# Opening, modulation schedule and norm placement of a two-block transformer kernel on one core

## The chip, the cores and the metric

The kernel runs on one core of a Trainium2 chip. The metric is the device time of one execution in microseconds (us), the median of three runs. The engines are TensorE (PE, products and transposes), VectorE (DVE), ScalarE (ACT), GpSimd (POOL, which here only issues DMAs) and SyncE (SP, which issues the weight DMAs).

## The reference

Two transformer blocks run one after the other on 256 tokens of width 1024, in float32. The first has two layers of "macaron" form, the second two layers on the same stream with a second (context) stream beside it.

```python
def first_block(x, c, ada_w, ada_b, norm_g, ...):
    c_act = jax.nn.silu(c)
    for l in range(2):
        mod = c_act @ ada_w[l] + ada_b[l]                    # 9 vectors of 1024 a layer
        sh1, sc1, g1, sh2, sc2, g2, sh3, sc3, g3 = jnp.split(mod, 9, axis=-1)
        n1 = modulate(rms_norm(h, norm_g[l, 0]), sh1, sc1)   # x * (1 + scale) + shift
        h = h + 0.5 * g1 * swiglu(n1, ...)                   # d_ff 2816
        n2 = modulate(rms_norm(h, norm_g[l, 1]), sh2, sc2)
        h = h + g2 * token_mixing(n2, ...)                   # two kinds of attention, gates, w_o
        n3 = modulate(rms_norm(h, norm_g[l, 2]), sh3, sc3)
        h = h + 0.5 * g3 * swiglu(n3, ...)
    return rms_norm(h, final_g)
# second block: layer 0 projects both streams with ev_w_in (1024 x 3104), runs gated scans;
# layer 1 is window attention; each with an MLP of 4096; its modulation vectors are
# silu(c) @ w_mod + b_mod and silu(c_ctx) @ w_mod + b_mod, 6 vectors of 1024 a layer and stream
```

## The kernel before, in words

**Weights.** Every weight matrix is cut into chunks of 1 MB (128 x 2048 float32). SP loads chunk n into `stage` (a ring of three), ACT rounds it into `whi`, DVE subtracts to get the rest `wlo` (both are `conv(n)`), and PE multiplies with both halves. A chunk of a projection is 48 products, of a feed-forward stage 32 wide pairs. The stages and their chunk counts stand in `PHASES`: F0 (first feed-forward), in0, gate0, out0 (token mixing), F1, F2, in1, gate1, out1, F3, then evc and evx (the "even inputs" of the context and the latent stream, 12 chunks each), evoc, evox, Mc, M0 (MLPs), odc, odx, odo, M1. DVE's conv of chunk n + 2 stands in window n of each stage, so DVE and ACT run two chunks ahead of PE, and each must wait until PE has used a chunk (`chunk_used`).

**Modulation vectors.** One vector is 8 steps on DVE: `mod_steps` multiplies a 128 x 1024 slice of the weight by a column of silu(c) and adds it to an accumulator (L1773, L1776). POOL loads the weight in quarters of 1 MB into `modw` (two buffers; the first eight, c = 0 to 7, have rooms of their own where possible) and one quarter feeds two steps. After 8 steps PE transposes the accumulator (`turn_mod`, 8 transposes, L742), and DVE sums and adds the bias (`take_mod`, L1784). The table `VECTORS` says which stage makes which vectors, `STEPS` and `EVEN_STEPS` how many steps stand in each window, `EVEN_TURNS` after which chunk of an even input PE turns a vector. PE stands still at a turn until DVE has done the 8 steps.

**Opening.** SP loads 11 rows of parameters and three small broadcasts (13 DMAs), ACT the identity, c, the other constants (772 KB) and x, POOL eight quarters: vector ada(0, 1) (the scale of the first norm) and ada(0, 0) (its shift). PE turns the parameters, turns x, sums the squares for the first norm (`rms_stat("n0")`), turns the scale vector, then the shift vector, and after `keep_warm` (products that keep PE busy, L633) the first chunk of F0.

**Norms.** A norm's mean square comes from 8 products with a matrix of ones (`column_sums`), whose squares ACT makes (`squares`) and whose root ACT and DVE take. n2 and n5 follow the out stages; the key n6 (the first block's last norm) is worked out inside evc, lc0 (a layer norm of the context stream) inside evx: this is the "other stream's norm" of the even inputs.

Of the kernel before, what the change touches and what calls it, by code (L numbers as in the profile page):

```python
# [42 lines left out]
def shape_constants():  # L43
# [21 lines left out]
    base = np.concatenate([ident, ones, blk, rot, sel_even, sel_odd, tri_f, tri_b, tri_s, pos_f, pos_b, cols], 1)  # L65
# [21 lines left out]
for _name, _width in (("ident", P), ("ones", P), ("blk", P), ("rot", P), ("sel_even", P), ("sel_odd", P),  # L87
                      ("tri_f", P), ("tri_b", P), ("tri_s", P), ("pos_f", T), ("pos_b", T), ("cols", 8)):
    CONST_AT[_name] = (_at, _width)
    _at += _width  # L90
BASE_W = _at
TABLE_W = 4 * T
# [25 lines left out]
def program(nc, A, out_ap, book):  # L118
    ctx = ExitStack()
    with ctx:  # L120
# [36 lines left out]
        hidden_table = same_room("hidden_table", "table", [P, 4 * 256], F32R)  # L157
        plain_xs = same_room("plain_xs", "xs", [P, KB, T], F32)
# [69 lines left out]
        def wmod(l, v, which):  # L228
# [11 lines left out]
            "out1": [ada(1, 8)],  # L240
            "F3": [wmod(0, 2, 2)] + [wmod(0, v, 1) for v in range(3)],
# [12 lines left out]
        NMOD = len(mods)  # L254

        def mc(key, k=0, n=1):
# [3 lines left out]

        macc_arena = arena[:, 43 * 256:47 * 256]
        macc_even = hid[:].rearrange("p s f t -> p (s f t)")[:, 0:1024]

        start_room = {c: arena[:, 4096 + 2048 * (c - 2):4096 + 2048 * (c - 1)] for c in (2, 3, 4)}
        start_room.update({5: nraw[:].rearrange("p b t -> p (b t)"), 6: stage[:, 2, :]})
        quarter = lambda c: start_room.get(c, modw[:, c % 2, :])
        macc_of = lambda m: macc_even if m == 1 or mod_first["evc"] <= m < mod_first["Mc"] else macc_arena
# [4 lines left out]
            "F1": [0] + 22 * [1] + 4 * [2] + [2, 0, 1, 1, 0, 0],  # L272
            "Mc": [0] + 15 * [1] + [1, 0, 2, 0, 0, 2, 2, 0, 0, 2, 2, 0, 2, 2, 2, 0],
            "M1": [0, 0] + 8 * [1] + 22 * [0],
            "out0": 4 * [0] + [2, 2, 2, 0],
        }
        for name, like in (("F2", "F0"), ("F3", "F1"), ("M0", "Mc"), ("out1", "out0")):
            STEPS[name] = STEPS[like]
        turn_at, step_n = {}, 16
        for name in ("F0", "in0", "out0", "F1", "F2", "in1", "out1", "F3", "evc", "evx", "Mc", "M0", "M1"):  # L280
# [31 lines left out]
        param_landed = sem("param_landed")  # L312
# [16 lines left out]
        nparam = 16 * (len(wide_rows) + 8)  # L329
# [74 lines left out]
        EVEN_TURNS = {"c": (4, 7, 10), "x": (4, 9)}  # L404
        EVEN_STEPS = {"c": (2, 0, 2, 2, 2, 2, 3, 3, 2, 3, 3, 0), "x": (2, 2, 2, 1, 1, 2, 2, 2, 1, 1, 0, 0)}
# [9 lines left out]
        def _(sp):  # L415
# [6 lines left out]
            for at, n, src in ((0, 16, A["od_sink_2"].rearrange("a h -> (a h)")), (16, 8, A["ev_ret_theta_2"].rearrange("a b c -> (a b c)")),  # L422
                               (24, 512, A["lam_p"].rearrange("a b c -> (a b c)"))):
                sp.dma_start(small[:, at:at + n], src.partition_broadcast(P)).then_inc(param_landed, 16)
# [21 lines left out]
            def ffn(name, l, i):  # L446
                n = first[name]
                g, u, d = A["ffn_wg"][l, i], A["ffn_wu"][l, i], A["ffn_wd"][l, i]
                for j in range(PAIRS):
                    load(n + 2 * j, cols(g, j))  # L450
                    load(n + 2 * j + 1, cols(u, j))
                    if name == "F0" and j == 0:
                        sp.wait_ge(mod_step, 14)
# [44 lines left out]
            sp.wait_ge(mod_step, 10)  # L498
# [32 lines left out]
        def _(pool):  # L531
            for m, (w, l, v, _, _, _) in enumerate(mods):
                for q in range(4):
                    c = 4 * m + q
                    src = w[l].rearrange("(k p) n -> p k n", p=P)[:, 2 * q:2 * q + 2, v * 1024:(v + 1) * 1024]
                    if c < 8:

                        if c == 7:
                            pool.wait_ge(mod_step, 4)
                        pool.dma_start(quarter(c).rearrange("p (a b) -> p a b", a=2), src).then_inc(start_landed[c], 16)  # L540
                        continue
# [3 lines left out]
                if m == 1:  # L545
                    pool.wait_ge(pe_out.sem, pe_out.at(("turned", 0)))
                    pool.wait_ge(mod_step, 12)
                    pool.dma_start(arena[:, 2048:4096].rearrange("p (a d) -> p a d", a=2),
                                   A["ctx_2"].rearrange("b (a p) d -> p (b a) d", p=P)).then_inc(ctx_landed, 16)
# [3 lines left out]
        def _(pe):  # L553
# [227 lines left out]
            def rms_stat(key):  # L781
# [3 lines left out]
                if key != "n0":  # L785
                    keep_warm(R[:, 1, :], 8 if key == "n1" else 16 if key in JOINED else 22)
# [23 lines left out]

            pe.wait_ge(param_landed, nparam)
# [3 lines left out]
            turn_rows(0)  # L815
            rms_stat("n0")
            pe.wait_ge(act_out.sem, act_out.at("cact"))
            turn_mod(0, R[:, 2:4, :])
            pe.wait_ge(mod_step, 14)
            pe.wait_ge(act_out.sem, act_out.at(("turned", 0)))  # L820
            keep_warm(Y[:, 0, :], 10)
            turn_mod(1, R[:, 2:4, :])
            keep_warm(Y[:, 0, :], 12)

            def mixer(l):
# [60 lines left out]
                for c in range(9):  # L886
# [9 lines left out]
                    if c == 3:  # L896
                        if l == 0:
                            pe.wait_ge(act_out.sem, act_out.at(("turned", 1)))
# [84 lines left out]
            def even(which):  # L983
# [6 lines left out]
                if which == "c":  # L990
                    column_sums(other)
                else:
                    mean_sums(other, other_res)
                for c in range(12):
# [4 lines left out]
                    if c == 1:  # L999
# [5 lines left out]
                        last.then_inc(pe_out.sem, pe_out.next(("lr", which)))  # L1005
                    if which == "x" and c == 3:
                        column_sums(other)
                    if c == 4:
# [252 lines left out]
        def _(act):  # L1261
# [27 lines left out]
            def ffn(name):  # L1289
# [22 lines left out]
                for w in range(24, 33):  # L1312
                    conv(n + w + 2)
                    if w == 28 and key is not None:
                        squares(key, resx, lambda h: (key, "res", h), (0, 1))
                    if w == 29 and name == "F3":
# [26 lines left out]
            def squares(key, src, ready, parts=range(4)):  # L1343
                if 0 in parts:
# [51 lines left out]
            def rms(key, target, l, i):  # L1396
                if key != "n0":
                    squares(key, resx, lambda h: (key, "res", h), (2, 3) if key in JOINED else range(4))
# [8 lines left out]
            act.dma_start(base[:, 0:P], A["const"][:, 0:P]).then_inc(ident_landed, 16)  # L1407
# [3 lines left out]
            act.dma_start(base[:, P:BASE_W], A["const"][:, P:BASE_W]).then_inc(param_landed, 16)  # L1411

# [3 lines left out]
            done(f(cact[:].rearrange("p a k -> p (a k)"), R[:, 2, 0:3 * KB], ACT.Silu), "cact")  # L1416
            def take_rows(s, res):
# [4 lines left out]
            squares("n0", resx, None)  # L1422
            root("n0", eps6)
            act.wait_ge(dve_out.sem, dve_out.at("lamdot"))
            done(f(stat[:, 0:4], stat[:, 0:4], ACT.Exp), "lamexp")
            act.wait_ge(dve_out.sem, dve_out.at("small"))
            link(f(ec("theta"), ec("theta"), ACT.Exp))
            done(f(ec("lg_all"), ec("theta"), ACT.Ln, scale=-1.0, bias=one), "lg")
            conv(0)
            conv(1)  # L1430

# [1041 lines left out]
```

## Time and profile before

| | |
|---|---|
| Median of 3 runs | 2349.35 us (2348.09 to 2349.47) |
| Profiled execution, its own time | 2350.69 us |
| Its span, first to last instruction | 2348.9 us |
| PE busy | 2227.6 us (95%) |
| DVE busy | 1771.9 us (75%) |
| ACT busy | 1155.4 us (49%) |
| DMA mean | 215 GB/s |

The profiled execution took 1.3 us longer than the median. PE is busy almost always, so what counts is the time in which it is not, and where it runs at the lower clock.

### The profile page before, as it was taken

What the parts mean: (1) busy time and instruction counts of PE and PEld (TensorE: products, weight loads), DVE (VectorE), ACT (ScalarE), POOL (GpSimd) and SP (SyncE); (2) the same over time, 40 slices, a digit from 0 to 9 for tenths busy, and PEclk for the clock granted to TensorE, in tenths of its full rate; (3) what the DMA queues carried; (4) which work ended last, traced back from release to release, by engine and by line L of the source; (5) the groups of instructions that cost most, each with busy time, mean ns of one, the idle gap of its engine ahead of it and who ended that gap; (6) DMA issues with size and microseconds to landing.
All of it is one profiled execution on the core that took longest, in us unless ns stands there. A gap on an engine that the chain in (4) does not pass through costs nothing.

```text
span 2348.9 us, 33801 instructions
## 1 busy us (share of the span) xinstructions
PE 2227.6 (95%) x14278; PEld 1943.2 (83%) x14294; DVE 1771.9 (75%) x2092; ACT 1155.4 (49%) x1443; POOL 109.5 (5%) x157
## 2 busy tenths in 40 slices
PE   4999999999999999999998788999999999999998
PEld 3888889788888889988888677878888888768886
DVE  6888776888788877688886676667878877686763
ACT  2554556444355455645534334436635733485742
POOL 1000000000000000000000000000000000000000
PEclk8999999999999999999999999999999999999999
DMA  8889654688878865458877515607778877304651
GB/s 309 269 279 320 216 180 144 200 275 286 279 233 279 300 227 180 154 189 277 278 268 243 208 52 187 214 19 251 256 263 271 277 242 259 108 3 146 211 195 56
DMA packets 330446, 505.22 MB, mean 215 GB/s; under 512 B 12327, under 2 KB 239878, under 8 KB 330295
## 3 DMA queue, kind: packets, MB, share of 16 engines
q1 hardware_dynamic: 288071, 340.70, 44.0%
q0 software_dynamic: 41616, 160.44, 19.7%
q8 instruction: 113, 1.85, 0.3%
q10 hardware_dynamic: 608, 1.92, 0.2%
q14 instruction: 38, 0.31, 0.0%
HBM read 501.98 MB, written 1.05 MB: 214 GB/s over the span
## 4 chain that ended last, share of the span: by engine, by line
PE 86%; DVE 8%; ACT 3%; issue 2%; DMA 1%; SPq 0%; ACTq 0%; DVEq 0%
PE banks L576 36%; PE banks L577 18%; PE banks L568 7%; PE banks L570 6%; PE banks L569 6%; PE banks L795 2%; PE banks L742 2%; PE banks L633 2%; PE banks L769 2%; DVE wlo L1749 1%; PE banks L778 1%; ACT whi L1283 1%; DVE hid L1776 1%; DMA arena<-in_lam_p_dram 1%; DVE arena L1776 0%
## 5 line engine op out<-in xcount | busy, mean ns | idle before, releaser
L1749 DVE TENSOR_TENSOR wlo<-stage,whi 128x2048 fp32r<-128x2048 f32 (+1 forms) x326 | 737.0, 2261 | 187.4 <-ACT whi L1283 186.7
L1283 ACT CAST whi<-stage 128x2048 fp32r<-128x2048 f32 x322 | 615.4, 1912 | 365.7 <-PE banks L577 281.9
L576 PE MATMUL banks<-xs,whi 128*128 128x512 f32 x2176 | 763.0, 396 | 3.0 <-DVE xs L1940 1.6
L577 PE MATMUL banks<-xs,wlo 128*128 128x256 f32 x2176 | 607.1, 279 | 0.0
L576 PEld LDWEIGHTS banks<-xs,whi 128*128 128x128 f32 x2176 | 408.2, 188 | 100.4 <-issue 2.9
L568 PE MATMUL banks<-xs,whi 128*128 128x256 f32 x1440 | 417.9, 290 | 11.6 <-DVE xs L1940 7.9
L577 PEld LDWEIGHTS banks<-xs,wlo 128*128 128x128 f32 x2176 | 410.0, 188 | 0.1
L569 PE MATMUL banks<-xs,whi 128*128 128x256 f32 x1440 | 409.1, 284 | 0.0
L570 PE MATMUL banks<-xs,wlo 128*128 128x256 f32 x1440 | 408.9, 284 | 0.0
L576 PE MATMUL banks<-hidden_arena,whi 128*128 128x512 f32 x992 | 354.3, 399 | 0.0
L568 PEld LDWEIGHTS banks<-xs,whi 128*128 128x128 f32 x1440 | 278.0, 193 | 22.5 <-issue 10.5
L1776 DVE SCALAR_TENSOR_TENSOR arena<-modw,cact,arena 128x1024 f32<-128x1024 f32 x220 | 281.8, 1281 | 9.3 <-DMA modw<-in_ada_w_dram 6.1
L577 PE MATMUL banks<-hidden_arena,wlo 128*128 128x256 f32 x992 | 278.8, 281 | 0.0
L569 PEld LDWEIGHTS banks<-xs,whi 128*128 128x128 f32 x1440 | 278.0, 193 | 0.9 <-issue 0.5
L570 PEld LDWEIGHTS banks<-xs,wlo 128*128 128x128 f32 x1440 | 277.7, 193 | 0.0
L576 PEld LDWEIGHTS banks<-hidden_arena,whi 128*128 128x128 f32 x992 | 186.5, 188 | 45.1
L577 PEld LDWEIGHTS banks<-hidden_arena,wlo 128*128 128x128 f32 x992 | 186.3, 188 | 0.1
L576 PE MATMUL banks<-hs,whi 128*128 128x512 f32 x336 | 120.3, 396 | 0.0
L544 POOL DMA_DIRECT2D modw<-in_w_mod_dram x80 | 57.1, 714 | 1174.7 <-DVE arena L1776 887.3
L577 PE MATMUL banks<-hs,wlo 128*128 128x256 f32 x336 | 94.0, 280 | 0.0
L544 POOL DMA_DIRECT2D modw<-in_ada_w_dram x64 | 45.7, 714 | 868.9 <-DVE arena L1776 846.2
L1303 ACT COPY hid<-banks 128x512 f32<-128x512 f32 x44 | 25.8, 587 | 120.1 <-PE banks L577 120.1
(320 smaller groups left out, 2492.6 us busy)
## 6 DMA issues: line engine op xcount, KB each, us to landing
stage<-in_mlp_w_dram SPq DMA_DIRECT2D x96, 1024.0 KB, 5.4
modw<-in_w_mod_dram POOLq DMA_DIRECT2D x80, 1024.0 KB, 5.8
modw<-in_ada_w_dram POOLq DMA_DIRECT2D x67, 1024.0 KB, 5.7
stage<-in_ffn_wg_dram SPq DMA_DIRECT2D x44, 1024.0 KB, 5.5
stage<-in_ffn_wu_dram SPq DMA_DIRECT2D x44, 1024.0 KB, 7.5
stage<-in_ffn_wd_dram SPq DMA_DIRECT2D x44, 1024.0 KB, 7.4
stage<-in_ev_w_in_dram SPq DMA_DIRECT2D x24, 1024.0 KB, 6.0
stage<-in_w_in_dram SPq DMA_DIRECT2D x18, 1024.0 KB, 5.7
```

Source lines behind the costliest of these rows:

```text
L544: pool.dma_start(modw[:, c % 2, :].rearrange("p (a b) -> p a b", a=2), src).then_inc(mod_landed[c % 2], 16)
L568: mm(out, hi, xh, start=first_mm, stop=False, skip_group_check=True)
L569: mm(out, hi, xl, start=False, stop=False, skip_group_check=True)
L570: return mm(out, lo, xh, start=False, stop=last_mm, skip_group_check=True)
L576: mm(out, hi, pair.rearrange("p a t -> p (a t)"), start=first_mm, stop=False, skip_group_check=True)
L577: return mm(out[:, 0:T], lo, pair[:, 0, :], start=False, stop=last_mm, skip_group_check=True)
L633: mm(bank, zero.to_broadcast([P, P]), zero.to_broadcast([P, 512]), start=True, stop=True)
L742: last = nc.tensor.transpose(banks[:, k // 4, (k % 4) * P:(k % 4 + 1) * P], macc_of(m)[:, k * P:(k + 1) * P], ident)
L769: last = mm(out, ones, src[:, k, :], start=k == 0, stop=k == 7, skip_group_check=True)
L1283: nc.scalar.copy(whi[:, s, :], stage[:, s, :]).then_inc(hi_done, 1)
L1749: last = v.tensor_tensor(wlo[:, s, at], stage[:, s, at], whi[:, s, at].bitcast(F32), ALU.subtract)
L1776: v.scalar_tensor_tensor(out=acc, in0=w, scalar=cc, in1=acc, op0=ALU.mult, op1=ALU.add).then_inc(mod_step, 1)
```

## The change

In the opening the shift vector is no longer made by DVE. Its four quarters stay where they land (two of them in rooms that are free then, `plain_hs` and `plain_xs`), and PE multiplies each 128 x 128 block by one column of silu(c), 64 products that add up in eight columns of one bank. DVE adds the bias. ACT loads x right after c and the rest of the constants only after conv(1). PE turns x first and the parameters after it, turns the scale vector ahead of the norm's sums, and conv(0) on ACT stands ahead of the norm's root. SP waits for quarter 3 before chunk 0, for quarter 5 before chunk 1 and for the end of the one-column products before chunk 2; POOL waits for that too before the context stream and the next quarters. Small scalar work moves into F0.

The out stages lose their six steps each to F1 and F3. Of evc's three vectors one goes to Mc, of evx's two one goes on; Mc and M0 have five vectors instead of four. ACT makes n2's and n5's squares bank by bank in the out stage, and `keep_warm` behind these norms is 16 instead of 22. The other stream's norm stands one or two chunks later in the even inputs, and the turns after chunks 5 and 9 (evc) and 9 (evx) instead of 4, 7, 10 and 4, 9.

```diff
         VECTORS = {
-            "start": [ada(0, 1), ada(0, 0)],
+            "start": [ada(0, 1)],
...
-            "out0": [ada(0, 8)],
-            "F1": [ada(1, v) for v in range(4)],
+            "F1": [ada(0, 8)] + [ada(1, v) for v in range(4)],
...
-            "evc": [wmod(0, v, 2) for v in range(3, 6)],
-            "evx": [wmod(0, 3, 1), wmod(0, 4, 1)],
-            "Mc": [wmod(0, 5, 1), wmod(1, 0, 2), wmod(1, 1, 2), wmod(1, 0, 1)],
-            "M0": [wmod(1, v, 1) for v in range(1, 5)],
+            "evc": [wmod(0, 3, 2), wmod(0, 4, 2)],
+            "evx": [wmod(0, 3, 1)],
+            "Mc": [wmod(0, 5, 2), wmod(0, 4, 1), wmod(0, 5, 1), wmod(1, 0, 2), wmod(1, 1, 2)],
+            "M0": [wmod(1, v, 1) for v in range(5)],
...
-            "Mc": [0] + 15 * [1] + [1, 0, 2, 0, 0, 2, 2, 0, 0, 2, 2, 0, 2, 2, 2, 0],
+            "Mc": [0] + 3 * [1, 1, 2, 1, 1] + [1, 0, 2, 2, 0, 2, 2, 2, 0, 2, 2, 0, 2, 2, 3, 0],
...
-        EVEN_TURNS = {"c": (4, 7, 10), "x": (4, 9)}
-        EVEN_STEPS = {"c": (2, 0, 2, 2, 2, 2, 3, 3, 2, 3, 3, 0), "x": (2, 2, 2, 1, 1, 2, 2, 2, 1, 1, 0, 0)}
+        EVEN_TURNS = {"c": (5, 9), "x": (9,)}
+        EVEN_STEPS = {"c": (1, 2, 2, 0, 2, 1, 2, 2, 2, 2, 0, 0), "x": (1, 1, 0, 1, 1, 0, 1, 1, 1, 1, 0, 0)}
...
+            keep_warm(Y[:, 3, :], 12)
+            turn_rows(0)
             pe.wait_ge(param_landed, nparam)
...
-            turn_rows(0)
-            rms_stat("n0")
             pe.wait_ge(act_out.sem, act_out.at("cact"))
             turn_mod(0, R[:, 2:4, :])
-            pe.wait_ge(mod_step, 14)
+            rms_stat("n0")
             pe.wait_ge(act_out.sem, act_out.at(("turned", 0)))
-            keep_warm(Y[:, 0, :], 10)
-            turn_mod(1, R[:, 2:4, :])
-            keep_warm(Y[:, 0, :], 12)
+            for t in range(8):
+                if t % 2 == 0:
+                    pe.wait_ge(start_landed[4 + t // 2], 16)
+                for k in range(KB):
+                    last = mm(Y[:, 0, k:k + 1], quarter(4 + t // 2)[:, (t % 2) * 1024 + k * P:(t % 2) * 1024 + (k + 1) * P],
+                              cact[:, 0, t:t + 1], start=t == 0 and k == 0, stop=t == 7, skip_group_check=True)
+            last.then_inc(pe_out.sem, pe_out.next("shift0"))
+            keep_warm(Y[:, 1, :], 12)
...
-            act.dma_start(base[:, P:BASE_W], A["const"][:, P:BASE_W]).then_inc(param_landed, 16)
...
             squares("n0", resx, None)
+            conv(0)
             root("n0", eps6)
...
-            conv(0)
             conv(1)
+            act.dma_start(base[:, FIRST_W:BASE_W], A["const"][:, FIRST_W:BASE_W]).then_inc(base_landed, 16)
...
                 for c in range(4, 8):
                     conv(n + c + 2)
+                    if c >= 5:
+                        squares(key, resx, lambda h: (key, "res", h), (c - 5,))
...
             def start_shift():
                 conv(0)
-                mod_steps(2)
-                take_mod(R[:, 2:4, :])
+                dve.wait_ge(pe_out.sem, pe_out.at("shift0"))
+                link(v.tensor_tensor(mc(shift0[5], 0, 8), Y[:, 0, 0:8], pcol[:, shift0[4]:shift0[4] + 8], ALU.add))
```

On PE the whole opening of before, up to the first product of F0 (L576; L795 are transposes of c, the parameters and x, L769 the norm's sums, L742 the turns of a modulation vector, L633 keep_warm):

```order
L795 MATMUL banks<-base,table 128x24
L795 MATMUL banks<-base,arena 128x49 x8
L795 MATMUL banks<-base,arena 128x7
L795 MATMUL banks<-base,arena 128x128 x16
L769 MATMUL banks<-resc,base 128x256 x8
L742 MATMUL banks<-base,arena 128x128 x8
L633 MATMUL banks<-base 128x512 x10
L742 MATMUL banks<-base,hid 128x128 x8
L633 MATMUL banks<-base 128x512 x12
L576 MATMUL banks<-xs,whi 128x512
```

and of the change (its lines are one or more further down; L826 are the one-column products, whose four rooms are the four quarters):

```order
L796 MATMUL banks<-base,table 128x24
L634 MATMUL banks<-base 128x512 x12
L796 MATMUL banks<-base,arena 128x128 x16
L796 MATMUL banks<-base,arena 128x49 x8
L796 MATMUL banks<-base,arena 128x7
L743 MATMUL banks<-base,arena 128x128 x8
L770 MATMUL banks<-resc,base 128x256 x8
L826 MATMUL banks<-cact,arena 128x1 x16
L826 MATMUL banks<-cact,plain_hs 128x1 x16
L826 MATMUL banks<-cact,stage 128x1 x16
L826 MATMUL banks<-cact,plain_xs 128x1 x16
L634 MATMUL banks<-base 128x512 x12
```

The scale vector's turn now stands ahead of the sums, and 64 one-column products stand where the shift vector's turn stood.

On DVE the middle of evc, before, from window 3 to the turn's take after chunk 7 (L1749 is the lo half of a chunk, L1773 and L1776 are steps, L1784 and L1786 the take of a vector, L2256 a part of the scan's gate):

```order
L1776 SCALAR_TENSOR_TENSOR hid<-modw,cact,hid 128x1024 x2
L1749 TENSOR_TENSOR wlo<-stage,whi 128x2048
L1776 SCALAR_TENSOR_TENSOR hid<-modw,cact,hid 128x1024 x2
L2256 SCALAR_TENSOR_TENSOR arena<-banks,arena 128x1024
L1749 TENSOR_TENSOR wlo<-stage,whi 128x2048
L1784 TENSOR_REDUCE mcol<-banks 128x8
L1786 TENSOR_TENSOR mcol<-mcol,pcol 128x8
L1773 TENSOR_SCALAR hid<-modw,cact 128x1024
L1776 SCALAR_TENSOR_TENSOR hid<-modw,cact,hid 128x1024
L1749 TENSOR_TENSOR wlo<-stage,whi 128x2048
L1776 SCALAR_TENSOR_TENSOR hid<-modw,cact,hid 128x1024 x3
```

and of the change, from the end of the norm (L1982 writes the normed stream) to the first steps of the second vector:

```order
L1982 SCALAR_TENSOR_TENSOR resx<-resx,pcol,arena 128x256 x8
L1761 TENSOR_TENSOR wlo<-stage,whi 128x2048
L1788 SCALAR_TENSOR_TENSOR hid<-modw,cact,hid 128x1024 x2
L2268 SCALAR_TENSOR_TENSOR arena<-banks,arena 128x1024
L1761 TENSOR_TENSOR wlo<-stage,whi 128x2048
L1788 SCALAR_TENSOR_TENSOR hid<-modw,cact,hid 128x1024
L1761 TENSOR_TENSOR wlo<-stage,whi 128x2048
L1796 TENSOR_REDUCE mcol<-banks 128x8
L1798 TENSOR_TENSOR mcol<-mcol,pcol 128x8
L1785 TENSOR_SCALAR hid<-modw,cact 128x1024
L1788 SCALAR_TENSOR_TENSOR hid<-modw,cact,hid 128x1024
```

The first vector's eighth step now stands one chunk later, alone in its window, and the norm stands right ahead of it.

## Rows read from the trace of the kernel before

**Rows 1.** The page, busy time of each engine over the span.

```profile
PE 2227.6 (95%) x14278; PEld 1943.2 (83%) x14294; DVE 1771.9 (75%) x2092; ACT 1155.4 (49%) x1443; POOL 109.5 (5%) x157
```

**Rows 2.** Stretches: us, busy of PE, PEld, DVE, ACT, POOL, PE clock, DMA share, GB/s.

```profile
8.00:19.00 11.00, 0.12 (x1) 0.00 (x0) 4.61 (x4) 0.19 (x1) 0.71 (x1) 1.00 0.98 377
...
1300.00:1350.00 50.00, 38.69 (x296) 35.15 (x299) 28.90 (x40) 17.30 (x20) 3.57 (x5) 0.90 0.53 186
```

**Rows 3.** Timeline of PE in the opening: start, length in us, idle before.

```profile
27.83 6.56 PE L769 MATMUL banks<-resc,base 128*128 128x256 f32 x16 [3.90 <-ACT resc L1357]
...
49.29 1.97 PE L742 MATMUL banks<-base,hid 128*128 128x128 f32 x8 [6.20 <-DVE hid L1776]
51.05 4.27 PE L633 MATMUL banks<-base 128*128 128x512 bf16 x12
54.97 0.58 PE L576 MATMUL banks<-xs,whi 128*128 128x512 f32 x1
```

**Rows 4.** DMA issues of the first 26 us: KB each, us to landing.

```profile
arena<-in_ada_w_dram POOLq DMA_DIRECT2D x3, 1024.0 KB, 18.1
...
arena<-in_x_dram ACTq DMA_DIRECT2D x1, 1024.0 KB, 14.4
...
base<-in_const_dram ACTq DMA_DIRECT2D x1, 772.0 KB
```

**Rows 5.** DMA queues from 1242 to 1244 us: packets, MB, share of 16 engines.

```profile
q0 software_dynamic: 131, 0.47, 60.4%
q1 hardware_dynamic: 289, 0.30, 42.5%
```

**Rows 6.** Groups on PE of the first 60 us, shapes apart: busy us, mean ns.

```profile
L795 PE MATMUL banks<-base,arena 128*128 128x128 f32 x16 | 3.3, 390 | 0.0
...
L795 PE MATMUL banks<-base,arena 49*128 49x49 f32 x8 | 1.1, 308 | 11.3 <-DMA arena<-in_lam_p_dram 11.3
```

**Rows 7.** Timeline of PE in the even inputs.

```profile
1237.55 5.38 PE L769 MATMUL banks<-arena,base 128*128 128x256 f32 x16 [2.71 <-ACT arena L1357]
...
1275.79 1.69 PE L742 MATMUL banks<-base,hid 128*128 128x128 f32 x8 [4.81 <-issue]
...
1300.13 1.97 PE L742 MATMUL banks<-base,hid 128*128 128x128 f32 x8 [4.44 <-DVE hid L1776]
...
1327.67 1.97 PE L742 MATMUL banks<-base,hid 128*128 128x128 f32 x8 [7.69 <-DVE hid L1776]
...
1422.80 3.62 PE L778 MATMUL banks<-resc,base 128*128 128x256 f32 x16
...
1464.69 1.94 PE L742 MATMUL banks<-base,hid 128*128 128x128 f32 x8 [6.77 <-issue]
```

**Rows 8.** Timeline of DVE in evc.

```profile
1270.88 2.29 DVE L1749 TENSOR_TENSOR wlo<-stage,whi 128x2048 fp32r<-128x2048 f32 x1 [2.33 <-ACT whi L1283]
...
1297.47 2.61 DVE L1776 SCALAR_TENSOR_TENSOR hid<-modw,cact,hid 128x1024 f32<-128x1024 f32 x2 [1.24 <-DMA modw<-in_w_mod_dram]
```

**Rows 9.** Waits of PE over the span: us in total, times, longest.

```profile
PE banks L766 <- ACT nraw L1351: 6.6, 2, 3.3
```

**Rows 10.** Timeline of PE at the norm n2 (end of out0).

```profile
435.73 0.59 PE L761 MATMUL banks<-nraw,base 128*128 128x256 f32 x2
...
442.79 6.63 PE L633 MATMUL banks<-base 128*128 128x512 bf16 x21 [0.22 <-issue]
449.07 0.58 PE L576 MATMUL banks<-xs,whi 128*128 128x512 f32 x1
```

**Rows 11.** Timeline of DVE at the norm n2.

```profile
434.80 2.60 DVE L1776 SCALAR_TENSOR_TENSOR arena<-modw,cact,arena 128x1024 f32<-128x1024 f32 x2
...
439.51 0.87 DVE L1902 SCALAR_TENSOR_TENSOR resx<-banks,ecol,resx 128x256 f32<-128x256 f32 x2
...
451.12 0.88 DVE L1996 SCALAR_TENSOR_TENSOR xs<-nraw,mcol,xs 128x256 fp32r<-128x256 f32 x2 [0.19 <-ACT xs L1390]
```

**Rows 12.** Timeline of DVE in Mc, after window 18.

```profile
1708.34 2.29 DVE L1749 TENSOR_TENSOR wlo<-stage,whi 128x2048 fp32r<-128x2048 f32 x1 [3.27 <-ACT whi L1283]
```

More of the change, by code:

```diff
@@ L91 @@
 BASE_W = _at
+FIRST_W = 2 * P + 8
 TABLE_W = 4 * T
@@ L785, in rms_stat @@
                 if key != "n0":
-                    keep_warm(R[:, 1, :], 8 if key == "n1" else 16 if key in JOINED else 22)
+                    keep_warm(R[:, 1, :], 8 if key == "n1" else 16)
             def ln_stat(key, res):
@@ L1005, in even @@
                         last.then_inc(pe_out.sem, pe_out.next(("lr", which)))
+                    if which == "c" and c == 1:
+                        column_sums(other)
+                    if which == "x" and c == 1:
+                        mean_sums(other, other_res)
                     if which == "x" and c == 3:
                         column_sums(other)
-                    if c == 4:
+                    if c == EVEN_TURNS[which][0]:
                         pe.wait_ge(dve_out.sem, dve_out.at((other, "rooted")))
@@ L1315, in ffn @@
                         squares(key, resx, lambda h: (key, "res", h), (0, 1))
+                    if w == 24 and name == "F0":
+                        act.wait_ge(base_landed, 16)
+                        act.wait_ge(dve_out.sem, dve_out.at("lamdot"))
+                        done(f(stat[:, 0:4], stat[:, 0:4], ACT.Exp), "lamexp")
+                        link(f(ec("theta"), ec("theta"), ACT.Exp))
+                        done(f(ec("lg_all"), ec("theta"), ACT.Ln, scale=-1.0, bias=one), "lg")
                     if w == 29 and name == "F3":
@@ L1343, in squares @@
             def squares(key, src, ready, parts=range(4)):
-                if 0 in parts:
+                if 0 in parts and key != "n0":
                     nc.scalar.preload_act_table_set(LN_EXP)
@@ L1565, in even @@
                         done(nc.scalar.copy(E["lr"][32:48, :], R[32:48, 3, 0:T]), ("lr", which))
-                        if which == "c":
-                            root(other, eps6)
-                    if c == 3 and which == "x":
+                    if c == 2 and which == "c":
+                        root(other, eps6)
+                    if c == 4 and which == "x":
                         root(other, eps5)
@@ L1819, in ffn @@
                     j = w // 2
+                    if name == "F0" and w == 2:
+                        lam_dots()
                     if w % 2 == 1:
@@ L1831, in ffn @@
                         residual_half(name, key, resx, lambda k: ec("g2x", k, 1), 0)
-                    if name == "F0" and w == 23:
+                    if name == "F0" and w == 26:
                         scalars()
@@ L2085, in _, with lam_dots @@
             done(v.tensor_copy(pcol[:, 8 * nwide:8 * nwide + 7], R[:, 1, 8 * nwide:8 * nwide + 7]), "pcol")
-            mod_steps(4)
             own("pcol")
             take_mod(R[:, 2:4, :])
-            mod_steps(2)
+            def lam_dots():
+                dve.wait_ge(small_landed, 48)
+                lam = small[:, 24:536].rearrange("p (x a n) -> p x a n", x=4, a=2)
+                prod = arena[:, 1700:1956].rearrange("p (x n) -> p x n", x=4)
+                link(v.tensor_tensor(prod, lam[:, :, 0, :], lam[:, :, 1, :], ALU.mult))
+                link(v.tensor_reduce(stat[:, 0:4], prod, AX_X, ALU.add))
+                v.tensor_scalar(ec("sink"), small[:, 0:16], -1.0, None, ALU.mult)
+                done(v.tensor_copy(ec("theta"), small[:, 16:24]), "lamdot")
             def scalars():
@@ L2243, in even @@
                     conv(n + c + 2)
-                    if which == "c" and c == 1:
+                    if which == "c" and c == 3:
                         final_norm(other)
-                    if which == "x" and c == 0:
+                    if which == "x" and c == 2:
                         ln_center(other, other_res)
-                    if which == "x" and c == 3:
+                    if which == "x" and c == 5:
                         ln_finish(other, other_res, 0, 0)
```

106 lines of the change are left out of this document (46 added, 60 removed).

## The prediction

> **What bounds the kernel now.** I read the page first: PE is busy for 2227.6 of 2348.9 us [rows 1]. The reader is to see that PE's 121 idle us are nearly all there is to win, beside the stretches in which it runs at its lower level. Stretches of 50 us show where they lie: the first 55 us, two gaps at the ends of the out stages, and the even inputs, where PE is busy for 38.7 of 50 us and the mean granted clock is 0.90, a mix of the levels 2.4 and 1.2 GHz [rows 2]. Elsewhere PE is all but full, and DVE has 6 to 10 us of 50 free there. Then the timelines of PE, DVE and ACT in these three places tell which wait ends last.
>
> In the opening it is this: PE sums the squares (6.56 us), stands until DVE has the shift vector's eight steps, turns it at 49.29, runs keep_warm, and F0's first product starts at 54.97 [rows 3]. In evc PE stands three times at a turn, 4.81, 4.44 and 7.69 us, and once, 2.71 us, for the squares of the other stream's norm; in evx once, 6.77 us [rows 7]. At n2 and n5 it stands for the last squares, 3.3 us each [rows 9].
>
> **Opening: what the change costs there.** The one-column products are the unknown. First, when may they begin? Of the DMAs, quarters 2 to 4 took 18.1 us in the median from issue (3.5 us), so quarter 3's landing was near 21.6 us; 772 KB of constants no longer go ahead of x and the quarters [rows 4], which at 377 GB/s [rows 2] is 2 us. So quarter 3 lands near 19.7, two steps of 1.3 each (two in 2.61, [rows 8]) end at 22.3, the turn (1.97, rows 3, at the lower clock, since PE has stood idle ahead of it) ends at 24.3, and the sums, 6.56 as before, at 30.9. x lands much earlier than its 17.3 (2.9 + 14.4) and isn't late for this.
>
> Then 64 float32 products. A float32 product has two rows in the trace (L769: 8 products, 16 rows), so 128 passes, each with its own load of 128 columns of weights. No row shows a one-column pass. The nearest are the float32 transposes of the opening [rows 6]: 128 columns wide 3.3 / 16 = 0.21 us each, 49 wide 1.1 / 8 = 0.14. The 79 columns between cost 0.07; one column would be 0.10 on that line, 0.14 if the load of the weights sets the pace from 49 columns on. I take 0.12: 128 x 0.12 = 15.4 us, end at 46.3. Bounds: 0.06, half of it, if PE is at its upper level (the transposes' pace fits the lower one), and 0.21, the widest row. Quarter 7 isn't late: the 11.6 MB of all quarters, x, parameters and two chunks take some 29 us at 377 to 400 GB/s behind a start of 4 us, so it lands near 33 to 35. From the turn's end (51.26) to F0's first product before were 3.7 us, set by keep_warm. So F0 starts near 50.0, **5.0 us earlier**. The other chain doesn't come last: chunk 0 lands at 30 to 34 (SP's small packets get 0.30 MB while POOL's get 0.47 [rows 5]), ACT's half of it ends two later, root, refinement, eight products and the lo half on DVE end near 41 to 44, and the first split needs 1.5 more.
>
> The Trainium skill, page "TensorE: Matmul & The Clock Gate", section "LDWEIGHTS (loading the stationary operand)", gives columns / 1.2 ns for a load of weights, 107 ns for 128 columns. By it 128 passes would be 13.7 us, a gain of 6.7. The section "Wait — 56ns, not 53.3ns?" of that page gives a floor of 25 ns, or 62 with decode in software; by that alone they would be 3 to 8 us.
>
> What the new waits give back: chunk 2 is asked for only at 46.3, together with chunk 3, the context stream and two quarters, 5 MB at once, where before chunk 2 was long there. By rows 5's shares chunk 2 lands near 54 and chunk 3 near 62. PE wants them 11.3 and 17 us after F0's start, at 61.3 and 67, with 4.2 us of ACT and DVE ahead of it, and DVE's small products (moved to window 2) and up-gate stand in between. Chunk 3 is late by about **1.5 us** (0 to 6); what hides the rest is PE's work on chunks 0 to 2.
>
> **evc.** Three gaps and the squares, 19.65 us [rows 7], go; the new order leaves two waits. Turn after chunk 5: DVE's lo half of chunk 6 starts at 1270.88 [rows 8] for the same reason as before (ACT's part of the gate). Behind it on DVE: itself 2.2, two steps 2.6, the gate's subtraction 1.2, the next lo 2.2, one step 1.3, so 1280.4. Chunk 4 ended at 1275.79 - 4.81 = 1270.98; a chunk is 6.0 us (from turn to turn 24.34, less 1.69 and 4.44, over three; 5.8 without the slow one behind a turn). So PE stands 3.5 us. Turn after chunk 9: the turn of before after chunk 7 stood 4.44 with three steps; one step less is 1.3, and 1.24 of it was a late quarter [rows 8], now asked for earlier: 1.7 left. So 14.4 us less idle. The sums took 5.38 where the same 16 passes took 3.62 in evx [rows 7], as they follow a gap: 1.8. Slow products behind a turn: about 0.7 each time, and one turn fewer with its 2.0: 4 in all with what goes at the gap removed. **evc: 20 us.** That the norm stands two windows later costs nothing: it is read only in evox's stage and its room only at the first turn, and DVE had 2.3 us idle in the place it takes and still ends ahead of ACT's late half.
>
> **evx.** 6.77 us idle, the turn 2.0, and a chunk that took 1.7 more at the lower clock behind them; left 0.3 to 0.6 at the turn after chunk 9 with one step in its window. **evx: 10 us.**
>
> **n2, n5.** Of n2: DVE's last residual starts at 439.51, though PE's last chunk ended at 435.73 (where the norm's own sums begin), because the pair sum waited for ACT's squares behind three casts, and two steps (2.60) and a lo half followed it [rows 10, 11]. With squares bank by bank and without steps it starts at 435.7: 3.8 less, and 0.6 more as the last sums follow no gap. keep_warm (6.63 for 21) ended later than the split was ready; with 16, and no lower clock, it ends before. The last piece of the split ended at 452.0 and then comes 4.4 earlier, 447.6, with two blocks' products (1.4) behind: the first chunk of F1 ends at 449.0 and not 449.07 + 5.65. **n2: 5.7**, n5 by its rows of the same kind (its sums were at the upper level) **4.7**.
>
> **What it moves.** 28 steps of 1.3 us go to F1, F3 (6 each), Mc and M0 (8 each), into windows with spare DVE time: in Mc, at window 19, DVE stood 3.27 us before its next lo half [rows 12] and gets two steps, 2.6. Their cover gone, each would cost 1.3. Not covered: the last window of Mc and M0, three steps for two just ahead of a turn, 1.3 each at most (I take 1.2); F3's window 30, 0.7; the two vectors' turns, 1.0 each at the upper level. **Loss 5.1 us.**
>
> **Sum**: 5.0 - 1.5 + 20 + 10 + 5.7 + 4.7 - 5.1 = 38.8, from 2350.69 is 2311.9; the profiled run was 1.3 over the median, so **2310.5 us**.
>
> **Rivals.**
> (A) One-column passes cost 0.2 or more, as wide transposes do. For it: PE does little in them, and all float32 transposes of the opening were slow; against: those move 128 columns through the array and these one. F0 then starts at 30.9 + 26.9 + 3.7 = 61.5, 6.5 later than before: sum 27, 2322.
> (B) Passes at 0.06 or less. The DVE chain then bounds, F0 at 43 to 45: 2304 to 2305. The skill's floor of 25 to 62 ns on the page named above would be this case.
> (C) The moved steps are not hidden: DVE is busy 39 to 44 of 50 us in those stages, and at half price they give 18 back: 2325. Against it: the idle 3.27 of rows 12, and two chunks of lead.
> (D) Slower than before: one-column passes don't overlap at all, since all add into one bank, and each takes its whole recorded length; L769's at the lower clock is 6.6 / 16 as pace but 0.31 to 0.6 as length (rows 6 have 0.31 and 0.39). At 0.6 they are 77 us, F0 starts at 111, 56 later: sum -17, 2368. It decides from (38.8 + 15.4) / 128 = 0.42 us a pass.
> (E) The change doesn't do it: the turns wait as long one chunk later, since steps and norm were only reordered. Then evc and evx give 10 in place of 30: 2330. Against it: steps per window ahead of each turn fell from three to two and one.
>
> **How the numbers follow.** My forecast 0.62, A 0.12, B 0.10, C 0.07, E 0.06, D 0.03. No more than 2 in 10 outside: 2300 to 2326 leaves out D, E and the far ends. Within 0.2% (4.7 us, about what a measurement of this kernel can tell from no change) of 2349.35 lies only a thin part of D and E: 0.02. Slower 0.02, faster 0.96.
>
> **What would show it.** Right: L826's rows about 0.12 apart; F0's first product near 50; PE's waits at turns in evc about 3.5 and 1.7, none of note in evx; n2's and n5's idle 3.3 gone; one small wait near F0's chunk 3. Wrong: passes far from 0.12, a wait of PE on lo halves in F0 over 6 us, or new waits at turns in Mc, M0, F1 or F3.

## The result, and the profile after

The changed kernel took 2335.81 us (median of 4 runs, 2334.38 to 2339.74), the kernel before, beside it, 2348.72 us. The ratio is 0.9942, 95% interval 0.9927 to 0.9957: by the ratio 13.6 us faster where 38.8 were forecast, and outside the range of 2300 to 2326. The profiled execution of the changed kernel was its longest, 2339.74 us with a span of 2338.0, so between the two spans lie 10.9 us.

To find where these went, I took the start of the same product in both timelines of PE and noted by how much the gap between the two kernels changed from one such mark to the next (positive is time saved):

| Stretch | Forecast | Measured |
|---|---|---|
| up to F0's first product (54.97, now 57.67) | 5.0 | -2.7 |
| F0's chunks 0 to 3 (fifth chunk 77.77, now 84.14) | -1.5 | -3.7 |
| n2 with the first two chunks of F1 | 5.7 | 5.5 |
| the rest of F1, up to n5 | 0 | -1.1 |
| n5 with the first two chunks of F3 | 4.7 | 4.0 |
| the rest of F3 | -0.7 | -1.9 |
| evc with its stage of scans | 20 | 20.3 |
| evx | 10 | 10.6 |
| evox | 0 | 1.9 |
| Mc | -2.2 | -9.4 |
| M0 | -2.2 | -10.2 |
| the rest | 0 | -2.4 |
| sum | 38.8 | 10.9 |

So the even inputs and the norms gave what was forecast. Of the 27.9 us between forecast and measurement 15.2 lie in the two MLPs, 7.7 in the stretch up to F0 and 2.2 in F0's first chunks. The page, busy time of each engine after:

```profile
PE 2243.5 (96%) x14388; PEld 1960.2 (84%) x14404; DVE 1759.6 (75%) x2083; ACT 1158.2 (50%) x1445; POOL 109.5 (5%) x157
```

PE's busy time grew by 15.9 us [rows 1]: a busy engine isn't a useful one, and 23.8 of it are the one-column products. The timeline of PE in the opening, to be laid beside [rows 3]:

```profile
23.92 1.94 PE L743 MATMUL banks<-base,arena 128*128 128x128 f32 x8 [6.45 <-DVE arena L1788]
25.65 4.12 PE L770 MATMUL banks<-resc,base 128*128 128x256 f32 x16
29.61 3.63 PE L826 MATMUL banks<-cact,arena 128*128 128x1 f32 x32
33.10 6.62 PE L826 MATMUL banks<-cact,plain_hs 128*128 128x1 f32 x32
39.58 6.97 PE L826 MATMUL banks<-cact,stage 128*128 128x1 f32 x32
46.41 6.96 PE L826 MATMUL banks<-cact,plain_xs 128*128 128x1 f32 x32
53.61 4.41 PE L634 MATMUL banks<-base 128*128 128x512 bf16 x11 [0.24 <-issue]
57.67 0.59 PE L577 MATMUL banks<-xs,whi 128*128 128x512 f32 x1
...
76.86 0.50 PE L577 MATMUL banks<-xs,whi 128*128 128x512 f32 x1 [1.90 <-DVE hid L1823]
```

The first 32 passes take 3.49 us from their start to that of the next ones, 0.109 us each; the other 96 take 0.20 to 0.22. Windows of 2 us on PE (us, busy, granted clock, DMA share, GB/s) show why:

```profile
30.00:32.00 2.00, 2.00 (x20) 1.00 1.08 359
32.00:34.00 2.00, 2.00 (x18) 0.87 1.10 350
34.00:36.00 2.00, 2.00 (x11) 0.50 0.49 156
...
44.00:46.00 2.00, 2.00 (x11) 0.50 0.00 0
```

PE is busy without a gap, and yet its granted clock falls from 2.4 to 1.2 GHz. The last number matters too: from 42 to 54 us the DMA queues are empty, since SP waits for these products before it asks for chunk 2.

The timeline of PE at the turns, beside [rows 7]: evc's two, evx's one, and the last ones of Mc and M0:

```profile
1275.69 1.72 PE L743 MATMUL banks<-base,hid 128*128 128x128 f32 x8 [3.72 <-issue]
...
1302.90 1.10 PE L743 MATMUL banks<-base,hid 128*128 128x128 f32 x8 [1.57 <-DVE hid L1788]
...
1466.53 1.06 PE L743 MATMUL banks<-base,hid 128*128 128x128 f32 x8 [0.29 <-issue]
...
1753.51 1.94 PE L743 MATMUL banks<-base,arena 128*128 128x128 f32 x8 [5.89 <-issue]
...
1952.85 1.94 PE L743 MATMUL banks<-base,arena 128*128 128x128 f32 x8 [6.17 <-issue]
```

The first three are as forecast (3.5, 1.7 and 0.3 to 0.6). The last two are new. DVE in windows 28 to 30 of Mc, just ahead of the first of them, beside [rows 12]:

```profile
1736.77 2.67 DVE L1788 SCALAR_TENSOR_TENSOR arena<-modw,cact,arena 128x1024 f32<-128x1024 f32 x2
1739.37 2.28 DVE L1761 TENSOR_TENSOR wlo<-stage,whi 128x2048 fp32r<-128x2048 f32 x1
1741.57 1.28 DVE L1788 SCALAR_TENSOR_TENSOR arena<-modw,cact,arena 128x1024 f32<-128x1024 f32 x1
1744.01 1.28 DVE L1788 SCALAR_TENSOR_TENSOR arena<-modw,cact,arena 128x1024 f32<-128x1024 f32 x1 [1.17 <-DMA modw<-in_w_mod_dram]
1745.21 2.29 DVE L1761 TENSOR_TENSOR wlo<-stage,whi 128x2048 fp32r<-128x2048 f32 x1
1747.41 1.28 DVE L1788 SCALAR_TENSOR_TENSOR arena<-modw,cact,arena 128x1024 f32<-128x1024 f32 x1
1750.80 2.60 DVE L1788 SCALAR_TENSOR_TENSOR arena<-modw,cact,arena 128x1024 f32<-128x1024 f32 x2 [2.11 <-DMA modw<-in_w_mod_dram]
```

Steps stand 2, 1 + 1, 1 + 2 here: the last vector had one step in window 26, so its first three quarters (two steps each) are split between two windows. And POOL, which issues the quarters:

```profile
1744.63 0.72 POOL L550 DMA_DIRECT2D modw<-in_w_mod_dram  x1 [5.56 <-issue]
```

`modw` has two rooms, so the last quarter can be asked for only when the step that ended at 1742.85 has freed one. It is asked for at 1744.63 and DVE has it at 1750.80, while PE has stood since 1747.62. In M0 the two waits for a quarter are 1.39 and 2.16 us.

### The profile page after: what moved, and what is told of

It reads as the page before. It is cut to its first block, busy times and chain, and to the rows that moved or that the text cites. A ratio compares the mean times of both kernels' runs of the same rounds, so it can differ in the third digit from the quotient of the medians.

```text
span 2338.0 us, 34014 instructions
## 1 busy us (share of the span) xinstructions
PE 2243.5 (96%) x14388; PEld 1960.2 (84%) x14404; DVE 1759.6 (75%) x2083; ACT 1158.2 (50%) x1445; POOL 109.5 (5%) x157
## 4 chain that ended last, share of the span: by engine, by line
PE 85%; DVE 9%; ACT 3%; issue 2%; DMA 1%; POOL 0%; ACTq 0%; DVEq 0%; SPq 0%; POOLq 0%
PE banks L577 35%; PE banks L578 18%; PE banks L569 7%; PE banks L571 7%; PE banks L570 7%; PE banks L796 2%; PE banks L743 2%; DVE wlo L1761 1%; PE banks L770 1%; PE banks L826 1%; PE banks L779 1%; PE banks L634 1%; DVE arena L1788 1%; DMA stage<-in_ffn_wu_dram 1%; DMA arena<-in_ada_w_dram 1%
## 5 line engine op out<-in xcount | busy, mean ns | idle before, releaser
L1788 DVE SCALAR_TENSOR_TENSOR arena<-modw,cact,arena 128x1024 f32<-128x1024 f32 x234 | 299.8, 1281 | 23.3 <-DMA modw<-in_w_mod_dram 15.7
```

The lines of the kernel that those rows point to most:

```text
L1788: v.scalar_tensor_tensor(out=acc, in0=w, scalar=cc, in1=acc, op0=ALU.mult, op1=ALU.add).then_inc(mod_step, 1)
```

## The experiments

Ratios are to the kernel before, run on the same chip beside each; the changed kernel's own is 0.9942. A hundredth is 23.5 us, and the intervals reach 0.0012 to 0.0015 to either side.

### The two halves of the change

**The opening undone** (that of before, with everything else as changed):

> The opening of before (shift vector by DVE, constants ahead of x), everything else as changed. Theory: the change's own opening costs time, F0's first product 2.7 us later and chunk 3 of F0 another 3.7 us, so this kernel is 6.4 us faster than the changed one: 2329.4 us, ratio to before 0.992. Rival: the opening gained what was forecast and the loss came from noise between programs: then this kernel is 3.5 us slower than the changed one, 2339.

Measured: 2331.25 us, ratio 0.9912 (0.9897 to 0.9927), F0's first product at 54.10, its fifth chunk at 76.48. The new opening costs some 7 us by the ratios and 7.7 by the fifth chunk's start (84.14): it lost time. The theory held.

**The other stream's norm at its old chunks**, steps and turns as changed:

```diff
                 first_chunk(n, R[:, 0, :], ("ev", which))
+                if which == "c":
+                    column_sums(other)
+                else:
+                    mean_sums(other, other_res)
...
-                    if which == "c" and c == 1:
-                        column_sums(other)
```

> The changed kernel with the other stream's norm back at its old chunks in evc and evx (sums behind chunk 0's first products, DVE's part in windows 1, 0 and 3), steps and turns as changed. Theory: of the 20 us that evc gained, the 2.7 us wait for the squares and some 1.8 us of slow products behind it come from the norm's place, the rest from steps and turns; so 4.5 us slower than the changed kernel, 2340, ratio 0.9961. Rival: the norm's later place is what shortened the waits at the turns, through DVE's windows: then 8 us or more are lost, ratio 0.998 or higher.

Measured: 2341.33 us, ratio 0.9965 (0.9953 to 0.9978), 5.4 us more than the change. The timeline of PE has the old wait again, while the turn's is where it was (3.72 in the changed kernel):

```profile
1236.20 3.69 PE L770 MATMUL banks<-arena,base 128*128 128x256 f32 x16 [2.71 <-ACT arena L1370]
...
1277.35 1.94 PE L743 MATMUL banks<-base,hid 128*128 128x128 f32 x8 [3.65 <-issue]
```

So of evc's 20 us the norm's place is worth about 4 (3.9 by the marks in PE's timeline, 5.4 by the ratios, whose intervals leave several us of room), and the turns the rest; evx saved as much in this kernel as in the changed one.

### The last turns of Mc and M0

**One step moved** from window 30 to window 1 of the changed kernel:

```diff
-            "Mc": [0] + 3 * [1, 1, 2, 1, 1] + [1, 0, 2, 2, 0, 2, 2, 2, 0, 2, 2, 0, 2, 2, 3, 0],
+            "Mc": [0] + [2, 1, 2, 1, 1] + 2 * [1, 1, 2, 1, 1] + [1, 0, 2, 2, 0, 2, 2, 2, 0, 2, 2, 0, 2, 2, 2, 0],
```

> The changed kernel with one step of Mc and M0 moved from window 30 to window 1, so that the last vector starts in window 26 with an even step and no quarter is split between two windows. Theory: the wait of 5.9 us at the last turn of each MLP comes from quarters that are asked for one window late (DVE waits 1.17 and 2.11 us for them) and the slow clock behind it; then 7 to 8 us come back in each of Mc and M0: 2320.5 us (2319 to 2324), waits at the last turns under 0.5 us. Rival: DVE has no time left there and the eight steps cost 1.3 us each wherever they stand: only the third step of window 30 is saved, 1.3 us twice, 2333.

Measured: 2319.88 us, ratio 0.987 (0.9856 to 0.9883): 17 us, by the ratios, from one step moved. The same turns in PE's timeline:

```profile
1747.08 1.06 PE L743 MATMUL banks<-base,arena 128*128 128x128 f32 x8 [1.58 <-issue]
...
1938.71 1.03 PE L743 MATMUL banks<-base,arena 128*128 128x128 f32 x8
```

The first still waits 1.58 where under 0.5 was expected: DVE's timeline has one wait for a quarter left there.

```profile
1744.37 2.61 DVE L1788 SCALAR_TENSOR_TENSOR arena<-modw,cact,arena 128x1024 f32<-128x1024 f32 x2 [1.25 <-DMA modw<-in_w_mod_dram]
```

By the marks Mc and M0 together now lose 4.2 us against the kernel before, where the change lost 19.6 and the forecast had 4.4.

**The kernel before, with the odd step and nothing else:**

```diff
-            "Mc": [0] + 15 * [1] + [1, 0, 2, 0, 0, 2, 2, 0, 0, 2, 2, 0, 2, 2, 2, 0],
+            "Mc": [0] + 15 * [1] + [1, 0, 2, 0, 0, 2, 2, 0, 0, 2, 1, 0, 2, 2, 3, 0],
```

> The kernel before, with one thing changed: in Mc and M0 the last vector has one step in window 26 and three in window 30, in place of two and two. The number of steps and vectors is that of before. Theory: what made the last turns of the changed kernel wait is that every quarter of the last vector is then split between two windows, so that quarter 3's room comes free a window late and its DMA lands after DVE wants it: a wait of about 4.6 us (1.17 and 2.11 for quarters and one step of 1.3) and 2 us of slow products behind it in each MLP, 13 us in all, ratio 1.0055. Rival: the waits came from the fifth vector, which leaves DVE too few free windows: then the one step in window 30 costs 1.3 us twice at most, ratio 1.001.

Measured: 2365.56 us, ratio 1.0058 (1.0045 to 1.007), 13.6 us slower than before. PE waits 5.03 and 4.41 us at the two turns, and DVE's timeline ahead of the first has the same two waits for a quarter as the changed kernel:

```profile
1772.56 1.28 DVE L1776 SCALAR_TENSOR_TENSOR arena<-modw,cact,arena 128x1024 f32<-128x1024 f32 x1 [1.11 <-DMA modw<-in_w_mod_dram]
...
1779.60 2.60 DVE L1776 SCALAR_TENSOR_TENSOR arena<-modw,cact,arena 128x1024 f32<-128x1024 f32 x2 [2.36 <-DMA modw<-in_w_mod_dram]
```

With four vectors and DVE no busier than before, moving one step from window 26 to window 30 makes the wait. The third step in window 30 accounts for 1.3 us of it, the two late quarters for the rest. The rival, too little free time on DVE, is out.

### The one-column products

**A wide product behind every fourth one-column product:**

```diff
+                    if (at * KB + k) % 4 == 3 and (at < 7 or k < 7):
+                        keep_warm(Y[:, 1, :], 1)
```

> The changed kernel with one product of keep_warm (128x512, bf16) behind every fourth one-column product. Theory: the granted clock falls from 1.00 to 0.50 some 4 us into the one-column products because they hardly use the array; with the wide ones it stays, the 128 passes take 0.109 us each as in the first quarter, 14.0 us and 15 x 0.22 = 3.3 us for the wide ones, in place of 23.8: F0 starts 6.5 us earlier, at 51.2, and the time is 2329. Rival: the clock falls all the same and the wide products come on top, 15 x 0.43 = 6.4 us: F0 at 64, 2342.

Measured: 2341.08 us, ratio 0.9957 (0.9945 to 0.997), 3.5 us slower than the change, which the two intervals alone can't tell from nothing. The timeline can: the clock fell all the same, to 0.53 from 34 us on and 0.50 from 36 on, and F0 began at 61.51, 3.8 us later. The rival held, though it had F0 at 64.

**Behind every one:**

> The changed kernel with one product of keep_warm (128x512, bf16) behind every one-column product, 63 in all, half of PE's time if the clock holds. Theory: the clock falls because one-column products count as little work; with half the time wide it holds at 1.00, and the stretch takes 14 + 63 x 0.22 = 27.9 us. Rival: something else pulls the clock down some 6 us after it rose, whatever PE does: then it is at 0.50 from 34 us on, as with every fourth, and the stretch takes over 45 us.

Measured: 2332.28 us, beside a kernel before of 2349.99; this is one run, so only its timeline is read. Windows of PE, the first as the clock had risen:

```profile
28.00:30.00 2.00, 2.00 (x11) 1.00 1.01 385
...
34.00:36.00 2.00, 2.00 (x19) 1.00 0.50 157
...
50.00:52.00 2.00, 2.00 (x19) 1.00 0.00 0
```

And PE's timeline at the end of the stretch:

```profile
52.43 0.28 PE L826 MATMUL banks<-cact,plain_xs 128*128 128x1 f32 x2
52.56 2.78 PE L634 MATMUL banks<-base 128*128 128x512 bf16 x12
55.00 0.58 PE L577 MATMUL banks<-xs,whi 128*128 128x512 f32 x1
```

The clock held at 1.00 throughout, so what pulled it down was the products' kind and not the time since it rose. PE's sequence repeats every 0.354 us; a wide product is 0.22 of that, which leaves 0.07 a pass, less than the 0.109 of a pass among its like. That part of the loads of weights lies behind the wide products would explain it, but isn't shown. The 64 products and 63 wide ones took 22.5 us, not the 27.9 expected, and end at 52.7, 0.7 us before the 64 alone in the changed kernel. keep_warm then takes 2.78 us, not 4.41, and F0 starts 2.7 us earlier, but then waits 2.95 us (1.90 before) for chunk 3, which comes from the next cause.

**Quarter 6 first, and chunk 2 asked for behind its 16 products:**

```diff
-            for t in range(8):
+            for at, t in enumerate((4, 5, 0, 1, 2, 3, 6, 7)):
...
+                if at == 1:
+                    last.then_inc(pe_out.sem, pe_out.next("quarter6"))
...
-                        sp.wait_ge(pe_out.sem, pe_out.at("shift0"))
+                        sp.wait_ge(pe_out.sem, pe_out.at("quarter6"))
```

> The changed kernel with quarter 6, which lies in chunk 2's room, multiplied first of the four, and SP waiting for those 16 products only before it asks for chunk 2. Theory: chunk 3's 1.9 us wait in F0 and the low clock behind it (3.7 us in all) come from chunk 2 being asked for at 53; now it is asked for near 34 and chunk 3 near 45, while the DMA queues are empty, and 3.7 us come back: 2332 us. Rival: the stall is that of ACT and DVE behind the first split, and nothing is gained: 2336. F0's first product stays near 57.7 in both.

Measured: 2332.26 us, ratio 0.992 (0.9906 to 0.9933). F0 starts at 57.21 and its fifth chunk at 80.58, 3.6 us ahead of the changed kernel's, with no gap of PE over 0.4 us in F0's first chunks. The theory held.

### Towards a better kernel

**Aligned steps and early chunk 2 together:**

> Aligned steps in Mc and M0, and quarter 6 first with the early request for chunk 2, together. The two stand at different places, so the savings should add: the ratios of the two alone were 0.987 and 0.992 against 0.9942 of the change, so 0.9848, 2315.5 us beside a kernel before of 2351.3. Rival: part of the saving of the early request was noise between programs: 0.987.

Measured: 2317.75 us, ratio 0.9865 (0.985 to 0.9879). F0's fifth chunk starts at 79.84, against 83.28 with aligned steps alone, so 3.4 us were saved there. The ratio moved by 0.0005 alone: its interval holds the rival's 0.987 and just misses the theory's 0.9848, so the time doesn't confirm that the savings add.

**DVE does half of the shift vector:**

```diff
-            for at, t in enumerate((4, 5, 0, 1, 2, 3, 6, 7)):
+            for at, t in enumerate((4, 5, 6, 7)):
...
+            pe.wait_ge(dve_out.sem, dve_out.at("shift_half"))
+            for k in range(KB):
+                last = mm(Y[:, 0, k:k + 1], macc_even[:, k * P:(k + 1) * P], ones[:, 0:1], start=False, stop=True, skip_group_check=True)
```

> As the one before, and DVE does the four steps of quarters 4 and 5 right behind its take of the scale vector, while PE multiplies quarters 6 and 7 and then DVE's accumulator by a column of ones: 40 products in place of 64, 80 passes. Theory: half the passes still run at the lower clock (0.21 us): the last one ends near 43.5 in place of 53, then DVE's own chain (lo half of chunk 0 to 44.3, then the split) and keep_warm bound, and F0 starts at 48 to 49 in place of 57: 8 us less, ratio 0.9815. Rival: DVE's steps start late, since its chain for the norm stands behind them, and PE waits: F0 at 52, ratio 0.983.

Measured: 2306.57 us, ratio 0.9819 (0.9804 to 0.9834), the fastest of all. PE's timeline:

```profile
28.98 3.63 PE L826 MATMUL banks<-cact,stage 128*128 128x1 f32 x32
32.47 6.20 PE L826 MATMUL banks<-cact,plain_xs 128*128 128x1 f32 x32
38.53 3.55 PE L832 MATMUL banks<-base,hid 128*128 128x1 f32 x16
42.32 4.84 PE L634 MATMUL banks<-base 128*128 128x512 bf16 x11 [0.24 <-issue]
46.66 0.73 PE L577 MATMUL banks<-xs,whi 128*128 128x512 f32 x1
```

F0 starts 11.0 us earlier than in the changed kernel. PE didn't wait for DVE, which had time while PE summed the squares.

**DVE does three quarters of it:**

> As the kernel in which DVE does half of the shift vector, but DVE does three of its four quarters (4, 5 and 7), PE multiplies quarter 6 alone (32 passes) and then DVE's accumulator by ones (16), keep_warm is 26 products, and DVE adds the bias ahead of its lo half of chunk 0. Theory: the shift vector is ready near 37, so ACT's split can start when DVE has normed the first blocks, at 41, and F0 starts at 43.7 in place of 46.7: 3 us less, ratio 0.9806. Rival: ACT's cast of chunk 1 and DVE's chain are no earlier and keep_warm's 26 products end after 46: no gain, 0.982.

Measured: 2308.88 us, ratio 0.9817 (0.9803 to 0.983): nothing gained. The shift vector was ready early, but PE stood 2 us for DVE's last step, the clock was at the lower level, and there keep_warm's products took 8.27 us, up to F0's start:

```profile
35.77 3.58 PE L832 MATMUL banks<-base,hid 128*128 128x1 f32 x16 [2.00 <-DVE hid L2106]
39.59 8.27 PE L634 MATMUL banks<-base 128*128 128x512 bf16 x25 [0.24 <-issue]
47.50 0.59 PE L577 MATMUL banks<-xs,whi 128*128 128x512 f32 x1
```

DVE's part of the split had begun at 44.23, 3.3 us before F0. My 26 products were sized for the upper level; with fewer it was not tried.

**evc's turns after chunks 6 and 10:**

```diff
-        EVEN_TURNS = {"c": (5, 9), "x": (9,)}
-        EVEN_STEPS = {"c": (1, 2, 2, 0, 2, 1, 2, 2, 2, 2, 0, 0), ...}
+        EVEN_TURNS = {"c": (6, 10), "x": (9,)}
+        EVEN_STEPS = {"c": (1, 2, 2, 0, 2, 1, 0, 2, 2, 2, 2, 0), ...}
```

> As the kernel in which DVE does half of the shift vector, with evc's turns after chunks 6 and 10 in place of 5 and 9, and no step in window 6, two in window 10. Theory: the 3.71 us at the first turn came from DVE's lo half, which waits for ACT behind the gate; one window later DVE has caught up, and only a wait like the 1.57 us at the second turn is left: 3.7 us and about 0.8 of slow products saved, ratio 0.980. Rival: the wait moves along to chunk 6 and 10, since the second vector's steps start a window later: 0.982 or higher.

Measured: 2308.23 us, ratio 0.9816 (0.9803 to 0.9829), the same. The first turn no longer waits, the second waits for both:

```profile
1261.39 1.03 PE L743 MATMUL banks<-base,hid 128*128 128x128 f32 x8
...
1291.75 1.97 PE L743 MATMUL banks<-base,hid 128*128 128x128 f32 x8 [6.30 <-DVE hid L1793]
```

**Both of the last two:**

> The two before it together. If both theories hold, 3 and 4.5 us less than the kernel in which DVE does half: ratio 0.9787. If neither, 0.982.

Measured: 2307.24 us, ratio 0.9815 (0.9802 to 0.9829). Nothing more.

## Why the prediction was wrong

**The price of a pass.** "I take 0.12: 128 x 0.12 = 15.4 us" is the first step that failed. The passes took 29.61 to 53.37, 0.186 us each on average, 8.4 us more. My 0.12 was meant for the lower level and came from a line through two widths of transposes, 0.21 for 128 columns and 0.14 for 49, on which fewer moved columns cost less; for the upper level I had half of it, 0.06. The passes took 0.20 to 0.22 at the lower level and 0.109 at the upper. That is what a transpose 128 columns wide takes: in the changed kernel those of the scale vector's turn (23.92) start 0.213 us apart at a granted clock of 0.50, those of x (14.72) 0.109 apart at 1.00. Moving one column in place of 128 saved nothing. My 0.14 was misread too: the 49-wide ones start 0.107 us apart, and their 1.1 us of busy time include the whole length of the last one. The second thing missed is which level it would be: it was 1.00 when these products began, and they brought it down while PE never stood. Had it held, 128 x 0.109 = 14.0 us would have been less than forecast.

Rival A had the lower level's price right and F0 at 61.5; it came at 57.67, since the first 32 passes ran at 0.109 (3.1 us less in all) and the first pass began 1.3 us earlier, against 0.6 more in keep_warm. Rival B never came: among their like no passes ran at 0.06. Rival D's sum doesn't follow from its price: at 0.6 a pass it would be 38.8 - 61.4, some 23 us slower than before and not 17; it didn't come either. The Trainium skill, page "TensorE: Matmul & The Clock Gate", section "LDWEIGHTS (loading the stationary operand)", gives columns / 1.2 ns for a load of weights, from which 107 ns for 128 columns is an estimate; the trace agrees with its 109 ns a pass at 2.4 GHz and not at 1.2 GHz, where a pass took twice that.

**Chunk 3's stall.** The mechanism was right, the size was 3.7 in place of 1.5 us: chunk 2 was asked for 7 us later than I thought, and a low clock of some 4 us stood behind the gap of 1.90. Asking earlier gave 3.1 of it back, and F0 itself began 0.5 earlier in that run.

**evc, evx.** 20.3 and 10.6 for 20 and 10, with waits of 3.72, 1.57 and 0.29 us where 3.5, 1.7 and 0.3 to 0.6 stood. "That the norm stands two windows later costs nothing" held, and its place saved about 4 of them. Rival E, the turns waiting as long as before, is out.

**n2, n5.** 5.5 and 4.0 for 5.7 and 4.7.

**The moved steps.** "Three steps for two just ahead of a turn, 1.3 each at most" is the second step that failed, and the costlier one: 9.4 and 10.2 us were lost in Mc and M0, where I had 2.2 each. I counted DVE's time and not the DMA behind it. The odd step split three quarters between two windows, so that the rooms for the next ones came free late; two waits of 1.17 and 2.11 us, with the third step, made a wait of 5.89 in Mc. There PE also stood 1.09 us for a lo half at 1741.71, ahead of the late quarters and not explained by them, and slow products followed (granted clock 0.50 to 1756, 0.70 to 1758). One step moved gave 17 us back, and the odd step alone cost the kernel before 13.6. Rival C (2325) had the place and the wrong reason. In F1 and F3, where the last vector's steps are even, little was lost; F3's last turn waits 1.17.

So A and C came both in part. My range took them one at a time: added up they would give 2310.5 + 11.5 + 14.5 = 2336.5. That this is near the measured 2335.81 is luck: what C counted, half of the price of all 28 moved steps, isn't what was lost in the MLPs.

## What to carry over

Before moving a step that feeds on a double buffer, write down in which window each buffer comes free and when its next DMA then lands: in the last vector two steps in a window kept these DMAs hidden, but for one wait of 1.25 us, and one step moved out of line exposed two. A product that moves one column cost here as much as one that moves 128 with the same size of weights, 0.109 us at 2.4 GHz and 0.21 at 1.2, and a run of such products brought TensorE's clock down although it was never idle. What paid was to give half of it to an engine with free time; wide products behind every one kept the clock up, but were tried in one run alone. And padding meant to keep the clock up takes twice as long while it runs at the lower level, 0.43 us a product against 0.22.

## What was not expected of the hardware

- TensorE was busy 2.00 of 2.00 us in each window from 34 us on and had a granted clock of 0.50; with a 128x512 product behind every one-column product it stayed at 1.00 for 22 us, with one behind every fourth it fell.
- The same two chunks of a feed-forward stage take 11.09 us in one stretch and 11.31 in another, at a granted clock of 1.00, and not in the same stretches of every execution: in F0 the kernel with the old opening had 11.09 and the kernel before 11.31. Over 17 such pairs that is 3.7 us a stage, the size of the scatter between runs; M1's first five pairs account so for 1.1 of the 2.4 us in the table's last row. What sets the pace stays open.
- In evox the changed kernel saved 1.9 us that no edit explains: PE's granted clock was 0.69 to 0.74 from 1548 to 1554 us in the kernel before. In the kernel before with the odd step, the same in this stage, it didn't fall there but 33 us earlier, so the place differs between executions.
